# A two-layer hybrid decoder trunk on one core: output projection in another order with banks of its own, and work around it moved

## What is computed

```python
h = x                                             # (1, 512, 1024) float32
for layer in range(2):
    hn = rms_norm(h, norm_mix_g[layer])
    # mixer: z = hn @ w_in, split in five sections of 512 columns (xa, gb, gc, xr, gr)
    # ya = gb * conv3(gc * xa)
    # yr = rg_lru(conv4(xr)) * gelu(gr)
    #      r, i = sigmoid(gate matmuls); a = exp(-8 r softplus(-lam)); h_t = a h_(t-1) + sqrt(1-a*a) i x
    # y  = group_rms_norm([ya, yr], g_mix, 64)
    # h += y @ w_out
    hn = rms_norm(h, norm_ffn_g[layer])
    if layer == 0:
        h = h + swiglu(hn, w1, w3, w2)            # hidden width 3072
    else:
        h = h + moe_swiglu(hn, router_w, ...)     # top 2 of 8 experts, hidden width 3584
return rms_norm(h, final_g)
```

## Time and profile before

| | |
|---|---|
| median of three runs | 2138.89 us (2136.17 to 2140.99) |
| the profiled execution | 2139.21 us |
| its span, first to last instruction | 2137.4 us |
| outside the span | 1.8 us |
| mean granted TensorE clock | 0.977 |
| PE busy | 2026.9 us (95%) |
| PE weight loads busy | 1761.8 us (82%) |
| DVE busy | 1545.8 us (72%) |
| ACT busy | 1218.7 us (57%) |
| POOL busy | 84.2 us (4%) |
| moved by DMA | 488.16 MB, mean 228 GB/s |

### The profile page before, as it was taken

How to read it: one execution, slowest core, us unless ns; L and a number is a source line. 1 busy time by engine, 2 the same in 40 slices (tenths; PEclk the granted TensorE clock), 3 DMA queues, 4 the chain that set the end, 5 groups by cost and what they waited for, 6 DMA issues and landing times.

```text
span 2137.4 us, 33175 instructions
## 1 busy us (share of the span) xinstructions
PE 2026.9 (95%) x10939; PEld 1761.8 (82%) x10940; DVE 1545.8 (72%) x1695; ACT 1218.7 (57%) x1554; POOL 84.2 (4%) x122
## 2 busy tenths in 40 slices
PE   6989999999999986999999999999999999999992
PEld 6767788888888765999999888888999888889992
DVE  6885666666678865666666688897666898986665
ACT  5342555555554423655655577777555777875553
POOL 1000000000000002000000000000000000000002
PEclk9999999999999987999999999999999999999996
DMA  7221856566653213777777699999775999997743
GB/s 238 96 67 40 285 184 187 176 198 188 193 154 123 79 51 123 244 236 242 252 234 238 208 368 365 371 388 334 242 239 188 358 380 358 392 359 240 239 149 132
DMA packets 245281, 488.16 MB, mean 228 GB/s; under 512 B 16564, under 2 KB 86308, under 8 KB 245236
## 3 DMA queue, kind: packets, MB, share of 16 engines
q1 hardware_dynamic: 237524, 461.52, 63.9%
q0 software_dynamic: 7568, 25.52, 3.5%
q10 hardware_dynamic: 144, 0.52, 0.1%
HBM read 473.20 MB, written 14.30 MB: 228 GB/s over the span
## 4 chain that ended last, share of the span: by engine, by line
PE 88%; DVE 6%; issue 3%; DMA 1%; ACT 1%; POOL 0%; DVEq 0%; POOLq 0%; ACTq 0%; SPq 0%
PE PS L1323 86%; DVE wlo L677 1%; DVE PS L776 1%; PE PS L1611 1%; DMA raw<-in_expert_w 1%; PE PS L1343 0%; ACT whi L347 0%; DVE OV L700 0%; DMA RES<-in_x 0%; POOL SM L1171 0%; DMA OV<-y_rows,addr 0%; DVE OV L905 0%; DVE XN L785 0%; DVE OV L751 0%; PE PS L1540 0%
## 5 line engine op out<-in xcount | busy, mean ns | idle before, releaser
L677 DVE TENSOR_TENSOR wlo<-raw,whi 128x1024 fp32r<-128x1024 f32 x882 | 1043.4, 1222 | 211.6 <-ACT whi L347 205.2
L347 ACT ACTIVATE whi<-raw 128x1024 fp32r<-128x1024 f32 x882 | 897.0, 1053 | 242.8 <-PE PS L1323 150.7
L1323 PE MATMUL PS<-XN,whi 128*128 128x352 f32 (+2 forms) x3328 | 982.5, 368 | 15.0 <-DVE OV L905 7.3
L1323 PE MATMUL PS<-XN,wlo 128*128 128x176 f32 (+2 forms) x2944 | 791.9, 269 | 2.1 <-issue 2.1
L1323 PEld LDWEIGHTS PS<-XN,whi 128*128 128x128 f32 x3328 | 622.7, 190 | 81.5 <-issue 15.0
L1323 PE MATMUL PS<-whi,XN 128*128 128x512 f32 x2272 | 671.1, 394 | 1.9 <-DVE XN L916 1.2
L1323 PEld LDWEIGHTS PS<-XN,wlo 128*128 128x128 f32 x2944 | 565.1, 192 | 13.0
L1323 PEld LDWEIGHTS PS<-whi,XN 128*128 128x128 f32 x2272 | 425.2, 188 | 96.4 <-issue 6.5
L1323 PE MATMUL PS<-wlo,XN 128*128 128x512 f32 x1248 | 424.0, 392 | 0.0
L1323 PEld LDWEIGHTS PS<-wlo,XN 128*128 128x128 f32 x1248 | 235.0, 188 | 50.7
L1323 PE MATMUL PS<-whi,hid 128*128 128x512 f32 x384 | 113.4, 397 | 4.0 <-DVE hid L864 4.0
(11 more groups left out here) (197 smaller groups left out, 932.6 us busy)
## 6 DMA issues: line engine op xcount, KB each, us to landing
raw<-in_expert_w SPq DMA_DIRECT2D x672, 512.0 KB, 5.0
raw<-in_ffn_w SPq DMA_DIRECT2D x144, 512.0 KB, 3.6
raw<-in_w_in SPq DMA_DIRECT2D x40, 512.0 KB, 5.2
raw<-in_w_out SPq DMA_DIRECT2D x16, 512.0 KB, 4.5
y_rows<-OV POOLq DMA_DIRECT2D x8, 512.0 KB, 5.8
y_rows<-OV POOLq DMA_DIRECT2D x1, 3072.0 KB, 12.9
RES<-in_x SPq DMA_DIRECT2D x4, 512.0 KB, 7.0
x_tok<-OV POOLq DMA_DIRECT2D x4, 512.0 KB, 3.3
```

The source lines that it names most:

```text
L347: act.activation(whi[:, u0 % CONV, half(h)], raw[:, r, half(h)], ACT.Copy).then_inc(s["hi_done"], 1)
L677: dve.tensor_tensor(wlo[:, w, half(h)], raw[:, u0 % RAW, half(h)], whi[:, w, half(h)].bitcast(F32), ALU.subtract).then_inc(s["lo_done"], 1)
L1323: return pe.matmul(out_, lhsT, rhs, start=start, stop=stop, skip_group_check=True)
```

## The change

- **Output projection.** Places are done in the order block 0 first four, block 1 first four, then two and two for each, then blocks 2 and 3 whole. `stat(l, 3)` follows block 0's first four places, writes banks 4 and 5 instead of 6 and 7, and waits for the last gate function of the layer (`ti_done`) instead of pair 2; `pair_root` and `pair_norm` of pair 3 work on these banks.
- **Block turns.** x_T of blocks 0 and 1 both stand after block 2, that of block 2 after block 3, in both layers; both wait for the normalization of pair 3. `norm` in ACT and DVE splits the turned blocks 0 and 1 after the squares and the scaling of block 2. In layer 1 x_T of blocks 2 and 3 each come one half tile later.
- **Unit split and silu table early.** Unit 16 and the silu table move from after the norm to inside it, ahead of the last turned block.
- **Zero rows in pieces.** Twelve DMAs in six steps, each step after four more hidden tiles. The gain and gate loads of layer 1 stand behind them on POOL.
- **Constants and first gate.** ACT and DVE split units 3, 4 and 5 of layer 0 later: ACT after one Exp, DVE after the first two convolutions. The parameters are turned one half tile pair earlier. The router weights lie in another place, and DVE makes their low part after the convolutions. `gate_mm(l, 0, 0)` stands between the two tiles of unit 2, in both layers. `gB` of the first norm is loaded by SP between blocks 1 and 2 of x, not by ACT.

```diff
@@
+        def stat_banks(p):
+            return slice(4, 6) if p == 3 else slice(6, 8)
@@ SP
             for b in range(TB):
                 sp.dma_start(RES[:, b, :], x[0, b * P:(b + 1) * P, :]).then_inc(s[f"x{b}"], 16)
+                if b == 1:
+                    sp.dma_start(gB, norm_mix_g[0].partition_broadcast(P)).then_inc(s["gB0_in"], 16)
@@ ACT, norm
                     squares(q * TB + b, junk[:, b % 2, :])
-                    if b:
-                        x_hi(q * TB + b - 1)
+                    for n in ((), (), (0, 1), (2,))[b]:
+                        x_hi(q * TB + n)
+                if q == 1:
+                    act.wait_ge(s["wout_done"], TB)
+                    split(FFN_BASE + 2, 0, 0)
+                    act.activation(warm, mhalf, ACT.Silu).then_inc(s["warm_up"], 1)
                 x_hi(q * TB + TB - 1)
@@ ACT, main
-                for i in range(2 if l == 0 else 3, CONV):
+                if l == 0:
+                    mix_split(0, 2)
+                    act.wait_ge(s["prm_ok"], 1)
+                    act.activation(lamw[:, 8:16], lamw[:, 0:8], ACT.Exp, scale=-1.0).then_inc(s["lam_exp"], 1)
+                for i in range(3, CONV):
                     mix_split(l, i)
@@ DVE, norm
-                    if b:
-                        x_lo(n - 1)
+                    for m in ((), (), (0, 1), (2,))[b]:
+                        x_lo(q * TB + m)
+                if q == 1:
+                    split(FFN_BASE + 2, 0)
@@ DVE, mixer, after the two convolutions
+                    if l + jj == 0:
+                        for i in range(3, CONV):
+                            mix_split(0, i)
+                        dve.wait_ge(s["rw_hi"], 1)
+                        dve.tensor_tensor(RW[:, :, E:2 * E], praw, RW[:, :, 0:E].bitcast(F32),
+                                          ALU.subtract).then_inc(s["rw_ok"], 1)
@@ POOL
-            zeros = gath[:, 0:1, :].broadcast_to([P, VIS - E, D])
-            pool.dma_start(y_v[0:P, E:VIS, :], zeros).then_inc(s["y_stored"], 16)
-            pool.dma_start(y_v[P:WIN, E:VIS, :], zeros[0:WIN - P]).then_inc(s["list_out"], 16)
+            zeros = gath[:, 0:1, :]
+            for j in range(VIS - E):
+                pool.wait_ge(s["w1_done"], F0 + 4 * (j + 1))
+                pool.dma_start(y_v[0:P, E + j:E + j + 1, :], zeros).then_inc(s["list_out" if j else "y_stored"], 16)
+                pool.dma_start(y_v[P:WIN, E + j:E + j + 1, :], zeros[0:WIN - P]).then_inc(s["list_out"], 16)
@@ PE, x_T
-                elif b == 0:
-                    pe.wait_ge(s["ti_done"], 2 * q + 2)
                 else:
                     pe.wait_ge(s["yn_done"], 4 * q + 4)
@@ PE, stat
-                if p:
+                if p == 3:
+                    pe.wait_ge(s["ti_done"], 4 * l + 4)
+                elif p:
                     pe.wait_ge(s["yn_done"], 8 * l + 2 * p)
@@ PE, mixer
                     z_tile(l, i, 0)
+                    if i == 2:
+                        gate_mm(l, 0, 0)
@@ PE, output projection
-                for b, places in ((0, range(6)), (1, range(6)), (0, (6, 7)), (1, (6, 7)), (2, range(8)), (3, range(8))):
+                for b, places in ((0, range(4)), (1, range(4)), (0, (4, 5)), (1, (4, 5)), (0, (6, 7)), (1, (6, 7)),
+                                  (2, range(8)), (3, range(8))):
@@
-                            if pos == 2:
-                                stat(l, 3)
@@
+                    if b == 0 and places[0] == 0:
+                        stat(l, 3)
                     if places[-1] == 7:
                         ins.then_inc(s["wout_done"], 1)
-                        if b:
-                            x_T(2 * l + 1, b - 1)
+                        for n in ((), (), (0, 1), (2,))[b]:
+                            x_T(2 * l + 1, n)
```

More of the change, by code:

```diff
@@ L144, in build_program @@
         slots, tokf = OV[:, 5376:5376 + WIN], OV[:, 5568:5568 + TB]
-        praw = OV[:, 5248:5312].rearrange("p (k e) -> p k e", k=KD)
+        praw = OV[:, 6784:6848].rearrange("p (k e) -> p k e", k=KD)
         e_T = PS[:, 2:4, :].rearrange("p a (k n) -> p (a k) n", n=P)
@@ L336, in _ @@
             act.activation(warm, mhalf, ACT.Square).then_inc(s["warm_up"], 1)
-            act.dma_start(gB, norm_mix_g[0].partition_broadcast(P)).then_inc(s["gB0_in"], 16)
             for n in ("c1_done", "sl_done", "c3_done", "hh_done"):
@@ L425, in pair_root @@
                 act.wait_ge(s["stat_done"], 4 * l + p + 1)
-                act.activation(PS[:, 6:8, :], PS[:, 6:8, :], ACT.Sqrt, bias=eps1).then_inc(s["rt_done"], 1)
+                v = PS[:, stat_banks(p), :]
+                act.activation(v, v, ACT.Sqrt, bias=eps1).then_inc(s["rt_done"], 1)
             def y_hi(l, t):
@@ L614, in _ @@
                     act.activation(RW[:, :, 0:E], praw, ACT.Copy).then_inc(s["rw_hi"], 1)
-                    act.wait_ge(s["prm_ok"], 1)
-                    act.activation(lamw[:, 8:16], lamw[:, 0:8], ACT.Exp, scale=-1.0).then_inc(s["lam_exp"], 1)
                     act.wait_ge(s["sp_ok"], 1)
@@ L622, in _ @@
                 norm(2 * l + 1, lambda b: (s["res_done"], l * TB + b + 1))
-                act.wait_ge(s["wout_done"], TB * (l + 1))
                 if l:
+                    act.wait_ge(s["wout_done"], 2 * TB)
                     for a, b in ((0, TB - 1), (TB - 1, TB)):
@@ L627, in _ @@
                         act.activation(LT[0:E, a * P:b * P], PS[0:E, a // 3, a * P:b * P], ACT.Copy).then_inc(s["log_sb"], 1)
-                for i in range(2, 3 if l == 0 else LEAD):
-                    split(nxt + i, 0, 0)
+                    for i in range(2, LEAD):
+                        split(nxt + i, 0, 0)
                 if l == 0:
-                    act.activation(warm, mhalf, ACT.Silu).then_inc(s["warm_up"], 1)
                     for h in range(2):
@@ L775, in pair_norm @@
                 dve.wait_ge(s["rt_done"], 4 * l + p + 1)
-                step(dve.reciprocal(PS[:, 6:8, :], PS[:, 6:8, :]))
+                v = PS[:, stat_banks(p), :]
+                step(dve.reciprocal(v, v))
                 for c in range(2):
@@ L779, in pair_norm @@
                     g = C_MG + 8 * l + t
-                    dve.scalar_tensor_tensor(Y[:, t, :], Y[:, t, :], prm[:, g:g + 1], PS[:, 6 + c, :], ALU.mult,
+                    dve.scalar_tensor_tensor(Y[:, t, :], Y[:, t, :], prm[:, g:g + 1], v[:, c, :], ALU.mult,
                                              ALU.mult).then_inc(s["yn_done"], 1)
@@ L977, in constants @@
             def constants():
-                dve.wait_ge(s["rw_hi"], 1)
-                dve.tensor_tensor(RW[:, :, E:2 * E], praw, RW[:, :, 0:E].bitcast(F32),
-                                  ALU.subtract).then_inc(s["rw_ok"], 1)
                 step(dve.tensor_scalar(prm2[:, 0:16], prm[:, C_BR:C_BR + 16], 0.5, None, ALU.mult))
@@ L1002, in _ @@
                     mix_split(0, 2)
-                    mix_split(0, 3)
                     dve.wait_ge(s["prm_T"], 1)
@@ L1006, in _ @@
                     dve.scalar_tensor_tensor(lamw[:, 0:8], lam, -1.0, lam, ALU.mult, ALU.max).then_inc(s["prm_ok"], 1)
-                    mix_split(0, 4)
-                    mix_split(0, 5)
                     constants()
@@ L1019, in _ @@
                 if l == 0:
-                    split(nxt + 2, 0)
                     for h in range(2):
@@ L1224, in _ @@
             blocks = ((0, P), (P, WIN))
-            zeros = gath[:, 0:1, :].broadcast_to([P, VIS - E, D])
-            pool.dma_start(y_v[0:P, E:VIS, :], zeros).then_inc(s["y_stored"], 16)
-            pool.dma_start(y_v[P:WIN, E:VIS, :], zeros[0:WIN - P]).then_inc(s["list_out"], 16)
+            zeros = gath[:, 0:1, :]
+            n_zero = 16 * (2 * (VIS - E) + 1)
+            for j in range(VIS - E):
+                pool.wait_ge(s["w1_done"], F0 + 4 * (j + 1))
+                pool.dma_start(y_v[0:P, E + j:E + j + 1, :], zeros).then_inc(s["list_out" if j else "y_stored"], 16)
+                pool.dma_start(y_v[P:WIN, E + j:E + j + 1, :], zeros[0:WIN - P]).then_inc(s["list_out"], 16)
             for a, b in blocks:
@@ L1234, in _ @@
             pool.wait_ge(s["y_stored"], 16)
-            pool.wait_ge(s["list_out"], 48)
+            pool.wait_ge(s["list_out"], n_zero)
             pool.sem_inc(s["zero_out"], 1)
@@ L1292, in _ @@
                                             tok[:, b:b + 1], None).then_inc(s["list_out"], 16)
-            pool.wait_ge(s["list_out"], 48 + 16 * 2 * TB)
+            pool.wait_ge(s["list_out"], n_zero + 16 * 2 * TB)
             for n, (a, b) in enumerate(blocks):
@@ L1383, in stat @@
                 pe.wait_ge(s["sq_done"], 4 * l + p + 1)
-                if p:
+                if p == 3:
+                    pe.wait_ge(s["ti_done"], 4 * l + 4)
+                elif p:
                     pe.wait_ge(s["yn_done"], 8 * l + 2 * p)
                 for c in range(2):
-                    ins = mm(PS[:, 6 + c, :], groups[:, :], sq[:, c, :], True, True)
```

(22 more changed lines are left out.)

6 lines of the change are left out of this document (removed).

## The result

The changed kernel takes 2116.53 us (median of 4 executions, 2114.42 to 2119.46) against 2138.52 (2136.17 to 2140.99) for the kernel before: a ratio of 0.9893, with a 95% interval of 0.988 to 0.9905, so 22 us off. The forecast was 2117.6, the range 2110 to 2125. The profiled execution took 2119.46 us, with a span of 2117.6 and a mean granted clock of 0.982 (0.977 before). That span is 19.8 us shorter than before's 2137.4.

What follows compares the result with a forecast made beforehand. PE, with 88% of the chain, bounds the kernel through its stops and lower clock in the mixers' ends and FFN's start. Layer 0's 12.6 plus layer 1's 10.3, less 1.6 for the clock, give 21.3 us off: 2117.6, range 2110 to 2125.

Steps and rivals of the forecast that it cites:

- The sum of layer 0: Layer 0 from start to FFN's `down`: DVE and PE times laid end to end, 12.6 us won.
- "I take 0" for gB: Kernel start, gB's load moved to SP's queue: 0 us, bounds -0.6 to +1.3.
- Constants and first gate: Layer 0 mixer's start: PE gains 4.0 us at unit 2, spent waiting; L820 comes 0.9 us late.
- Zero rows ... 0: FFN: the old burst made PE stop nowhere, so spreading the zero rows out gives 0 us.
- the gain of the FFN's start: Layer 0, `up` to `down`: stop falls from 3.71 to 0.8 us and `down` runs at the upper clock.
- Layer 1: Layer 1's mixer: 0.9 earlier at L820, 7.8 to block 3's end, 1.6 for the clock; 10.3 us won.
- 1.6 us charged for the clock behind the four stops left: Both layers, remaining stops of 2.2 and 1.4 us: the clock may drop, 1.6 us charged once.
- Rival A: Both mixers: the clock falls behind every stop left, four times 1.6 us, 2122.4 us; chance 0.13.
- The table load: Layer 0 FFN's start: 1.28 us by the row, kept over the skill's 2.66; at most 0.8 us more stop would go.
- B: Layer 0's mixer: DVE isn't late as loads land fast, up to 4.9 us better, 2112.7; chance 0.06.
- C: Layer 0's mixer: loads land late or DVE loses counted slack, 5 us worse, 2122.6; chance 0.06.
- E: Projection: PE stays at its lower clock, slower, 2204 us at worst, 2159 with blocks 0 and 1 alone; chance 0.03.

Runs made afterwards that it cites:

- e1: Changed kernel with the first norm's gain (gB) loaded on ACT's queue again; 2115.82 us, 0.9884 of the kernel before.
- e4: Changed kernel with constants, low parts of units 3 to 5, parameter turn and first gate product in their old places; 2114.27 us, ratio 0.987 to the kernel before.
- e7: Changed kernel with gB on ACT's queue and DVE's low parts of unit 3 (layer 0) ahead of the convolutions; 2113.12 us, 0.9872 of the kernel before.
- e6: Changed kernel with the zero rows written in two large DMAs again; 2122.13 us, 0.9915 of the kernel before.
- e11: Kernel before with unit 16 and the silu table early and the zero rows in pieces; 2130.60 us, ratio 0.9953.
- e5: Kernel before with only unit 16 and the silu table early; 2139.90 us, ratio 0.9996.
- e10: Kernel before with only the zero rows in pieces; 2141.68 us, ratio 1.0003.
- e8: Kernel before with the projection's order, pair 3's banks and the later turns together, nothing else; 2120.64 us, ratio 0.9902.
- e2: Kernel before with only the projection's order and pair 3's banks 4 and 5; 2130.61 us, ratio 0.9951.
- e3: Kernel before with only the later turns in projection and norm; 2131.42 us, ratio 0.9951.

## Why the prediction was right, and where not

Every kernel here computes the whole of the reference, so the times compare as they stand.

- **The sum of layer 0.** Forecast and trace: L764 at 61.4 and 61.80; L820 at 147.4 and 147.94; stop ahead of place 7 2.2 and 1.74; block 2 at 176.3 after 1.4 and 176.63 after 0.95; block 3's end 200.0 and 200.31; `up` 201.3 and 201.83; `down` at 214.3 to 214.4 after 0.8 and 214.79 after 0.55. Layer 0 as a whole: 12.6 and 12.3 (616.34 - 604.04). Of the 0.5 us at `up`, 0.3 are there at block 3's end; the other 0.2 are in the sum itself, which put `up` 1.3 us behind block 3, where both traces have 1.5. What made this close is that DVE's instructions were laid end to end, with PE's stops as the result and not as the start of the sum.
- **"I take 0" for gB** was off by 0.1 to 1.0 us at the first `z`, within the bound of +1.3. At `up` nothing of it is left that e1 can tell.
- **Constants and first gate.** The step that said PE's 4 us are spent waiting for DVE is right, and e4 bears it out: undoing the constants and the gate product costs nothing in the median. What the step lacked is the other side. A gap of 3.5 us on DVE, ahead of the convolutions, was there to be filled, and e7 turned it into 4.9 us at `up`.
- **"Zero rows ... 0"** is the step that failed in its reasoning. The argument was that PE's only stop under the burst was DVE's 3.71 us, so the burst was harmless. But that stop and the low clock behind it were the cover, and another line of the same prediction took the cover away. e6 prices it: 6.8 us from `up` to the FFN's end, 5.6 in the median. In the sum the zero came out right, since the change brought the pieces too; the gain of the FFN's start, 5.5 us in the prediction and 5.8 in e11, is in truth one of two edits together and of neither alone (e5, e10).
- **Layer 1.** 10.3 forecast, 11.0 measured (224.85 - 213.87). About 2.2 of this is the clock, for the two kernels whose layer 1 is that of before and where it didn't fall behind the 2.09 us stop (e5 and e11) take 222.53 and 222.67. The 1.6 that I had for that stop was right: from the turn behind it to the experts the kernel before takes 58.1 us, e5 and e11 56.5. The other 0.6 to 0.7 lie between `stat` and that turn (25.9 us before, 25.1 and 25.3), behind the stop of 6.8 us: the prediction took layer 0's rows for both layers, and in layer 0 this stretch was 25.1 us before. The rest is stops.
- **1.6 us charged for the clock behind the four stops left.** In the profiled execution nothing of this is seen: both windows above have 1.00, and block 2, from 761.31 in layer 1, is as long as in layer 0 (772.37 - 761.31 = 11.06; 187.65 - 176.63 = 11.02). Without the charge the sum is 22.9 and the medians differ by 22.0, against 21.3 with it, so the charge made the total neither better nor worse by much. Rival A is out. The rule behind it in the Trainium skill (TensorE: Matmul & The Clock Gate, A second HAM failure mode: psum-queue depth-cycling) is that brief idle times between groups of matmuls, where they come often enough, make the clock go up and down. Here the trace doesn't agree for stops as short as those left: with stops of 1.90, 1.74 and 0.95 us the window stays at 1.00. It does for longer ones: stops of 2.1 to 2.8 us lowered the clock in some executions and not in others, those of 3.7 us and more, in the mixers and the FFN, lowered it in every trace.
- **The table load.** It takes 1.28 us at 205.74 and the next function starts at 207.03, so no drain shows in this trace, and PE's 0.55 us ahead of `down` end with DVE's last sum. The Trainium skill, ScalarE: Activation LUTs, What ACT_TABLE_LOAD costs, has 2.66 us with the drain; the row decides. It bore on nothing, as the load has gone from the path.
- **B, C, E** did not come about: DVE was neither early nor late by more than 0.6 us against the forecast, and the clock was at 1.00 through the projection.

The prediction came within 1.1 us of the median for the right reasons in the mixers, and with one reason short in the FFN; that the two edits of the FFN came in one change, so that the wrong zero did no harm, was luck. What it could not have told is the experts' stage, which alone moves a single execution by up to 6 us.

## What to carry over

Before a burst of stores is called free, ask what hides it and whether the same change takes that away: here two edits were worth nothing each and 5.8 us of the FFN together. When an order of work is changed, read the stops in a row, not one by one: taking 6.8 us away from `stat` made the next stop grow from 2.09 to 4.44. And look for the gaps of the engine that is now late, upstream of where it is late: 2.3 us of work moved into a gap gave 4.9 at `up`, probably since loads and another engine hung on it.

## What the hardware showed that I had not expected

- The clock behind a stop of 2 to 3 us is not the same from execution to execution of equal code. Behind 2.82 us ahead of the first gate product it stayed up in the kernel before, e8 and e11 (1.98 us for the product); it fell in e2, e4, e5 and e10 (3.78 us), and for a part of the product in e3 (2.70 us). The same holds for 2.1 us: the turn behind it took 1.07 us for eight in the kernel before (layer 0) and 1.72 (layer 1). Behind stops of 3.7 us and more, in the mixers and the FFN, it fell in every trace, but not by the same amount: the twelve matmuls behind 3.7 to 3.8 us took 4.2 to 5.3 us instead of 2.75, and `stat` behind 6.8 us 3.70 to 3.75 instead of 1.88. Falls and their length make 4.4 of the 5.05 us between e10 and e11. What decides it I did not find.
- Behind the 4.1 MB burst from POOL's queue (3072 and 1152 KB, landed after 12.9 and 16.7 us in the kernel before) a weight half of 512 KB on SP's queue took up to 15.3 us to land before, 19.1 in e6 and 19.5 in e5, and ACT stood up to 9.2 and 9.6 us for one in the last two. With the stores cut to 512 KB and fewer, the median is 4.1 us and the longest 4.4.
- The experts' stage varies by 6 us over the 14 executions in the table (1293.6 to 1299.7), though no edit touches it; its cause stays open.
